# Block 1's attention scores: queries stacked as high over low part, keys in both halves of the rows, two products a score for three

## The chip, the core and the metric

The kernel runs on one core of a Trainium2 chip. The core has five engines with a queue of instructions each: TensorE (PE, matrix products, with its weight loads shown apart as PEld), VectorE (DVE), ScalarE (ACT), GpSimd (POOL) and SyncE (SP, which here only issues transfers, DMAs). Engines wait for each other by semaphores. The metric is the device time of one execution in microseconds (us), lower is better.

## What is computed

A transformer block (block 1) and then two layers of a second kind (block 2), on 512 positions of width 1024, all in fp32. The change lies in block 1's attention. Cut to what matters:

```python
z = rms_norm(x, norm_mix) @ w_in
q_a, k_a, v_a, q_b, k_b, v_b, g_a, g_b = split(z)
# A: 8 heads of 64 over 2 key heads, 512 positions, window of 128 to either side
sc = einsum('bqkgd,bskd->bkgqs', qi, ki) * scale - slopes * dist   # masked, with a sink
y_a = softmax(sc) @ vi
# B: 8 heads of 64 with 8 key heads, each position sees 16 columns of every row of an 8 x 64 grid
sc = einsum('bchd,brckhd->bhcrk', qr, kn) * scale + bias
y_b = softmax(sc) @ vn
x = x + (sigmoid(g_a + b) * (y_a @ w_proj_a) + sigmoid(g_b + b) * (y_b @ w_proj_b)) @ w_out
```

## The kernel before, in words

**Precision.** Every fp32 operand of a product is kept as two fp32r numbers, a high part (an ACT copy, rounded) and a low part (DVE: value less high part). A product of two such operands is three matmuls, high x high, high x low and low x high (`PASSES`), added up in PSUM.

**Stages of block 1.** First the projections of x (0 to 109 us in the trace): weight slabs of 256 columns go into two raw buffers (`K.raw`, slab j into buffer j % 2), are split by ACT (L915) and DVE (L1217) into two weight buffers `K.w`, and PE multiplies them (`fm`, L1741). `IN_TILES` lists 18 tiles: four of A's queries (qa), A's values and keys (va, ka), four of B's queries (qb), B's values (vb) and keys (kb). DVE scales each tile into `K.t` (L1256), ACT writes its high part (`in_hi`, L959) and DVE its low part (`in_lo`, L1230), all 128 rows at once. A tile of queries holds two heads: head 2t in rows 0 to 63, head 2t+1 in rows 64 to 127. `K.ka` holds the two key heads of A in the same way, `K.kb` tile t B's key heads 2t and 2t+1.

Then attention (109 to about 210 us), with A's eight heads before B's eight, each in four tiles of 128 queries, 64 tiles in all, numbered n. A tile of A has 256 keys (first and last of a head) or 384, one of B 256. Tile n goes through all engines: PE scores S (`scores(n)`, L1723) into one of two banks; DVE adds the bias and takes the maximum (L1355); ACT exponentiates (L977); DVE takes the reciprocal of the sum (L1361); POOL multiplies by it (L728); PE transposes (L1826); ACT copies the high part (L1015) and DVE makes the low part (L1381); PE multiplies two tiles at once with the values (`values`, L1853, nine matmuls). After a head, ACT (L986) and DVE (L1373) write its output over the queries' tile.

**The order** is written out by hand and fixed on every engine. PE runs scores(n+3), transposes(n), and for odd n the values of tiles n-3 and n-2. DVE runs scores(n+3), for n = 4h+6 the output of head h, the reciprocal of n+2, the low part of n. ACT runs that same output first, then the exponential of n+2, then the high part of n. POOL runs probabilities(n) and, in B's second to seventh head, after each of the first three tiles an addition of B's bias and mask for the next head (L777, `masked`). Scores 0, 1, 2 and 3 are issued around and inside the last projection tile.

The scores multiply with 64 active rows, `r = slice(e * HD, (e + 1) * HD)` with e the parity of the head.

**SP's queue**, in order: slabs 6 to 8, slab 9 (columns GA0), slab 10 (GB0), which waits until slab 8 is split and so raw buffer 0 is free; eight transfers of A's bias (`biasa`, L646), from the third on each waiting for the scores of the head two before; six of B's bias (`rawb`, L632), each waiting for the masks two heads before; then, after all values, the merge's slabs. Slab 10 is split by ACT and DVE in the merge, after attention.

Of the kernel before, what the change touches and what calls it, by code (L numbers as in the profile page):

```python
# [19 lines left out]
P = 128  # L20
# [146 lines left out]
def allocate(nc, ctx, K):  # L167
# [3 lines left out]
    def semaphore(name):  # L171
        return ctx.enter_context(nc.semaphore(name))
# [51 lines left out]
    def at(name, kb, shape, dt, start=None):  # L224
        off = (a0 if start is None else start) + kb * 1024
        return nc.alloc_sbuf_tensor_at(name, shape, dt, offset=int(off))
# [9 lines left out]
    K.rt = at("rt", 6, [P, 2, 2 * P], F32, p0)  # L236

    K.qa = at("qa", 0, [P, 2, HALF, SEQ], F32R)
    K.ka = at("ka", 16, [P, 2, SEQ], F32R)
    K.va = at("va", 20, [P, 2, TT, P], F32R)  # L240
    K.qb = at("qb", 24, [P, 2, HALF, SEQ], F32R)
    K.kvb = at("kvb", 40, [P, 2 * 2 * HALF * SEQ], F32R)
    n = 2 * HALF * SEQ
    K.kb = K.kvb[:, 0:n].rearrange("p (h t s) -> p h t s", h=2, t=HALF)
    K.vb = K.kvb[:, n:2 * n].rearrange("p (h t s) -> p h t s", h=2, t=TT)
# [48 lines left out]
    K.group_lo = semaphore("group_lo")  # L294
    K.fold_ok = semaphore("fold_ok")
    K.va_full = semaphore("va_full")
    K.pt_zero = semaphore("pt_zero")
    K.tile_full = semaphore("tile_full")
    K.tile_out = semaphore("tile_out")
# [89 lines left out]
def in_dest(K, to, part):  # L389

    name, t = to
    if name == "qa":
        return K.qa[:, part, t, :]
    if name == "qb":
        return blocks(K.qb[:, part, t, :])[:, ::-1, :, ::-1]
    if name == "kb":
        return K.kb[:, part, t, :]
    if name == "ka":
        return K.ka[:, part, :]
    if name == "va":  # L400
        return K.va[:, part, :, :]
    return K.vb[:, part, :, t * P:(t + 1) * P]


def in_shape(to, ap):
# [6 lines left out]
def blocks(ap):  # L412


    return ap.rearrange("p (b r c) -> p r b c", r=KH, c=BLOCK)
# [113 lines left out]
def program_sync(nc, sp, K):  # L529
    a = K.a  # L530

    def slab(j, pieces, pairs=None):


        sp.wait_ge(K.w_lo, (j - 1 + QA_MORE if (j - 3).k >= 0 else Num(HALF)).value())
        if pairs is not None:
            sp.wait_ge(K.pv_done, pairs.value())
        inc = 64 // len(pieces(K.raw[:, j % 2, :]))
        for dst, src, *n in pieces(K.raw[:, j % 2, :]):
            sp.dma_start(dst, src).then_inc(K.w_in_sem[j % 2], n[0] if n else inc)  # L540
# [86 lines left out]
    def bias_rows(h):  # L627


        per = (2 * KH - 1) * WINDOW  # L630
        src = bass.AP(K.rows.tensor, h * per, [[WINDOW, KH], [HEADS * per, BLOCK], [1, KH * WINDOW]])
        sp.dma_start(K.rawb[h % 2][:, :, :], src).then_inc(K.biasb_in[h % 2], 16)  # L632
# [4 lines left out]
    for j in range(6, 9):  # L637
        in_slab(j)
    slab(Num(J_MERGE), columns(a["w_in"][0], GA0))
    slab(Num(J_MERGE + 1), columns(a["w_in"][0], GB0))  # L640

    for h in range(HEADS):
        if h >= 2:
            sp.wait_ge(K.s_taken, S_A + TT * (h - 1))
        head = (h % 2) * HALF + h // 2
        sp.dma_start(K.biasa[:, h % 2, :], a["alibi"][head]).then_inc(K.biasa_in[h % 2], 16)  # L646
    for h in range(2, HEADS):
        sp.wait_ge(K.biasb_ok, 3 * (h - 1))
        bias_rows(h)
    sp.wait_ge(K.pv_done, HEADS * TT)  # L650

    for i in range(4):
# [251 lines left out]
def program_act(nc, act, K):  # L904
# [153 lines left out]
    square_of(KT - 1)  # L1058
    def in_hi(k):
        _, _, form, to = IN_TILES[k]  # L1060
        if form == "turn":
            act.wait_ge(K.va_full, turns(k) + 1)
            hi(in_dest(K, to, 0), in_shape(to, K.T[turns(k) % 2][:, :]))
        else:
            act.wait_ge(K.tile_out, Num(G_IN + k + 1).value())
            hi(in_dest(K, to, 0), in_shape(to, in_src(K, k)))
# [145 lines left out]
def program_vector(nc, dve, K):  # L1212
# [230 lines left out]
    def in_lo(k):  # L1443
        _, _, form, to = IN_TILES[k]
        src = K.T[turns(k) % 2][:, :] if form == "turn" else in_src(K, k)
        lo(in_dest(K, to, 1), in_shape(to, src), in_dest(K, to, 0), Num(H_IN + k))

    def in_normed(k):
# [270 lines left out]
def program_pe(nc, pe, K):  # L1719
# [72 lines left out]
    def attention(A, meanwhile=None):  # L1792
# [3 lines left out]
        def scores(n):  # L1796
            t, e, i, b0, b1 = A.where(n)
            h, kind = n // TT % HEADS, A.at(n)
            r = slice(e * HD, (e + 1) * HD)
            w = (b1 - b0) * P  # L1800
            qs = slice(i * P, (i + 1) * P)
            pe.wait_ge(K.s_taken, (S + n - 1).value())
            if kind == "B" and A.at(n - 1) == "A":
                pe.wait_ge(K.split_lo, H_MERGE)
            if kind == "A":
                pairs = [(K.qa[r, p, t, qs], K.ka[r, q, b0 * P:b1 * P]) for p, q in PASSES]
            elif kind == "B":
                keys = [blocks_of(K.kb[r, q, t, :])[:, B_KEYS[i]] for q in range(2)]
                pairs = [(K.qb[r, p, t, qs], keys[q]) for p, q in PASSES]
            else:  # L1810
                if i == 0:
                    pe.wait_ge(K.tile_out, (A.g_qk(h) + 2).value())
                pairs = [(K.qkh[0:QK, h % 2, 0, p, qs], K.qkh[0:QK, h % 2, 1, q, :]) for p, q in PASSES]
            dst = K.S[(S + n) % 2][:, 0:w]
            if kind == "B":
                dst = dst.rearrange("p (o r c) -> p o r c", r=KH, c=BLOCK)
            product(dst, pairs, K.s_full)
# [323 lines left out]
```

## Time and profile before

| | us |
|---|---|
| median of 3 runs | 1511.17 (1510.67 to 1511.65) |
| profiled execution, its own time | 1508.71 |
| its span, first to last instruction | 1506.7 |
| PE busy | 1482.9 (98%) |
| DVE / ACT / POOL busy | 807.1 / 617.9 / 359.5 |
| PE, share of the chain that ended last | 90% |

The profile is of one execution. Its rows give for each group of instructions the engine, the line, what is written and read, the count, and times in us from the start of the span. A row of the timeline merges neighbours of one kind: its length reaches from the start of the first to the end of the last, and since matmuls are pipelined, the start of the next row is the better measure of how long a group held PE. The granted clock is the share of TensorE's full 2.4 GHz.

### The profile page before, as it was taken

The numbers are of one execution on the slowest core, as the hardware profiler recorded it, in microseconds if no ns is written. First come the engines' busy times: TensorE is split into PE (matmuls) and PEld (weight loads), VectorE is DVE, ScalarE is ACT, GpSimd is POOL, SyncE is SP. The second block draws the span as 40 slices with busy tenths as digits, with TensorE's granted clock in tenths as the row PEclk, the third lists the DMA queues.
The fourth block names the chain that finished last, engine by engine and source line by source line (L and its number), as shares of the span: only waits on it lengthen the run. The fifth ranks groups of instructions, "written<-read, shape, count | busy, mean of one in ns | idle before, by whom it ended". The sixth has DMA issues, their size and how long they took to land.

```text
span 1506.7 us, 18810 instructions
## 1 busy us (share of the span) xinstructions
PE 1482.9 (98%) x7141; PEld 1226.0 (81%) x7141; DVE 807.1 (54%) x1318; ACT 617.9 (41%) x947; POOL 359.5 (24%) x362
## 2 busy tenths in 40 slices
PE   9999999999999999999999999999999999999998
PEld 7887788888888888888888777888888878888886
DVE  6447754344443434344578685544446879644344
ACT  5326752233422323234434675332333458533232
POOL 2104540002100000001308495210120747320012
PEclk9999999999999999999999999999999999999999
DMA  6531022323232232323232002323224200232321
GB/s 199 108 95 33 16 63 86 110 85 122 84 112 84 87 108 84 111 84 112 63 112 84 1 1 85 112 84 109 87 73 129 73 13 1 85 112 84 112 84 57
DMA packets 136478, 125.96 MB, mean 84 GB/s; under 512 B 20807, under 2 KB 132687, under 8 KB 136399
## 3 DMA queue, kind: packets, MB, share of 16 engines
q1 hardware_dynamic: 136239, 124.83, 26.6%
q8 instruction: 51, 0.84, 0.2%
q14 instruction: 28, 0.23, 0.0%
q10 hardware_dynamic: 160, 0.07, 0.0%
HBM read 122.75 MB, written 2.39 MB: 83 GB/s over the span
## 4 chain that ended last, share of the span: by engine, by line
PE 90%; DVE 4%; POOL 4%; ACT 1%; issue 1%; DMA 0%; DVEq 0%; ACTq 0%; SPq 0%; POOLq 0%
PE G L1741 73%; PE G L1723 5%; PE S L1723 4%; PE T L1826 2%; PE G L1853 2%; POOL t L728 2%; PE G L1913 1%; DVE sq L1355 1%; PE G L1846 1%; DVE ab L1234 1%; POOL w L838 1%; DVE pt_l L1381 0%; DMA raw<-in_w_in 0%; DVE z L1369 0%; POOL qk L826 0%
## 5 line engine op out<-in xcount | busy, mean ns | idle before, releaser
L1741 PE MATMUL G<-gx,w 128*128 128x512 f32 x3024 | 694.2, 390 | 0.2 <-DVE w L1217 0.2
L1741 PEld LDWEIGHTS G<-gx,w 128*128 128x128 f32 x3024 | 566.6, 188 | 119.9 <-issue 1.9
L1217 DVE TENSOR_TENSOR w<-raw,w 128x2048 fp32r<-128x2048 f32 (+1 forms) x110 | 252.9, 2299 | 224.1 <-ACT w L915 224.1
L915 ACT ACTIVATE w<-raw 128x2048 fp32r<-128x2048 f32 x112 | 211.6, 1889 | 135.4 <-PE G L1741 109.4
L1741 PE MATMUL G<-kvb,w 128*128 128x512 f32 x960 | 218.4, 389 | 0.0
L1741 PEld LDWEIGHTS G<-kvb,w 128*128 128x128 f32 x960 | 180.2, 188 | 37.4
L728 POOL TENSOR_TENSOR t<-t,rden 128x512 f32<-128x512 f32 (+2 forms) x128 | 108.8, 853 | 142.9 <-DVE rden L1361 142.3
L785 POOL TENSOR_TENSOR t<-sig 128x512 f32<-128x512 f32 x24 | 35.3, 1473 | 356.7 <-DVE sig L1429 356.7
L1486 DVE TENSOR_TENSOR x<-G,x 128x512 f32<-128x512 f32 x56 | 38.6, 689 | 115.3 <-PE G L1741 115.3
L977 ACT ACTIVATE t<-sq,nm 128x512 f32<-128x512 f32 (+3 forms) x128 | 80.2, 627 | 23.2 <-DVE nm L1355 22.6
L866 POOL TENSOR_TENSOR sumsq_f<-sumsq_f,sq_f 128x512 f32<-128x512 f32 x7 | 9.1, 1299 | 333.4 <-ACT sq_f L945 333.4
L1741 PE MATMUL G<-m,w 128*128 128x512 f32 x384 | 87.4, 389 | 0.0
L1741 PEld LDWEIGHTS G<-m,w 128*128 128x128 f32 x384 | 72.1, 188 | 15.0
L1256 DVE SCALAR_TENSOR_TENSOR sig<-G,rstd 128x512 f32<-128x512 f32 x48 | 33.0, 687 | 94.5 <-PE G L1741 94.5
L1826 PE MATMUL T<-ident,t 128*128 128x128 f32 x400 | 69.5, 285 | 11.3 <-POOL t L728 11.3
L1826 PEld LDWEIGHTS T<-ident,t 128*128 128x128 f32 x400 | 44.0, 140 | 37.2 <-POOL t L728 23.3
L1022 ACT ACTIVATE sig<-sig,lp 128x512 f32<-128x512 f32 x32 | 23.2, 724 | 107.6 <-DVE sig L1256 107.6
L719 POOL TENSOR_TENSOR sumsq<-sumsq,sq 128x512 f32<-128x512 f32 x28 | 37.7, 1346 | 119.7 <-ACT sq L933 104.2
L1099 ACT ACTIVATE sq<-t 128x512 f32<-128x512 f32 x32 | 20.2, 632 | 110.8 <-DVE t L1509 110.8
L1723 PE MATMUL S<-ab 96*128 96x512 f32 x192 | 57.7, 410 | 0.7 <-DVE nm L1355 0.7
L1381 DVE TENSOR_TENSOR pt<-T,pt 128x256 fp32r<-128x256 f32 (+2 forms) x96 | 50.6, 527 | 8.0 <-ACT pt L1015 5.1
L1429 DVE TENSOR_TENSOR sig<-G,sig 128x512 f32<-128x512 f32 x48 | 32.0, 686 | 40.9 <-PE G L1741 40.9
(228 smaller groups left out, 1761.2 us busy)
## 6 DMA issues: line engine op xcount, KB each, us to landing
raw<-in_w_in SPq DMA_DIRECT2D x98, 512.0 KB, 7.5
raw<-in_w_up SPq DMA_DIRECT2D x32, 512.0 KB
raw<-in_w_down SPq DMA_DIRECT2D x32, 512.0 KB
raw<-in_w_out SPq DMA_DIRECT2D x24, 512.0 KB
raw<-in_w_attn_proj SPq DMA_DIRECT2D x8, 512.0 KB
raw<-in_w_fourier_proj SPq DMA_DIRECT2D x8, 512.0 KB
xin<-in_x SPq DMA_DIRECT2D x4, 512.0 KB, 6.9
raw<-in_w_proj_a SPq DMA_DIRECT2D x8, 256.0 KB
```

Source lines behind the costliest of these rows:

```text
L719: nc.gpsimd.tensor_tensor(K.sumsq[:, :], K.sumsq[:, :], K.sq[:, k % 2, :], ALU.add).then_inc(K.sum_ok, 1)
L728: nc.gpsimd.tensor_tensor(p, p, K.rden[:, n % 4:n % 4 + 1].broadcast_to([P, (hi - lo) * P]), ALU.mult).then_inc(K.probs_ok, 1)
L785: nc.gpsimd.tensor_tensor(K.t[:, m, :], sig[:, m, :], sig[:, 2 + m, :], ALU.add).then_inc(K.mix_ok, 1)
L915: nc.scalar.activation(K.w[:, j % 2, 0, 0:n], K.raw[:, j % 2, 0:n], ACT.Copy).then_inc(K.w_hi, 1)
L977: nc.scalar.activation(K.t[:, n % 3, 0:width], K.sq[:, n % 2, 0:width], ACT.Exp, bias=K.nm[:, n % 4:n % 4 + 1], scale=-1.0, accum_out=K.de ...
L1217: nc.vector.tensor_tensor(K.w[:, s, 1, 0:n], K.raw[:, s, 0:n], K.w[:, s, 0, 0:n].bitcast(F32), ALU.subtract).then_inc(K.w_lo, 1)
L1256: part = nc.vector.scalar_tensor_tensor(out=dst, in0=src, scalar=scale, in1=rstd, op0=ALU.mult, op1=ALU.mult)
L1381: nc.vector.tensor_tensor(K.pt[A.at(n)][m % 2][:, 1, b0:b1, e, :], K.T[(U + n) % 2][:, 0:(b1 - b0) * P].rearrange("p (k c) -> p k c", c=P) ...
L1486: nc.vector.tensor_tensor(K.x[:, k, :], psum(g)[:, :], K.x[:, k, :], ALU.add).then_inc(K.tile_out, 1)
L1723: mm = nc.tensor.matmul(bank, lhs, rhs, start=(i == 0), stop=(i == len(pairs) - 1))
L1741: mm = nc.tensor.matmul(b[:, :], w(p, k), x(q, k), start=(k == i == 0), stop=(k == kts - 1 and i == len(PASSES) - 1))
L1826: mm = nc.tensor.transpose(K.T[(U + n) % 2][:, k * P:(k + 1) * P], K.t[:, n % 3, c:c + P], K.ident[:, :])
```

## The change

Queries are stored in another way: for head 2t+e, `qsa[:, e, t, :]` (and `qsb`) holds its 64 high-part rows in its own half of the 128 rows and its 64 low-part rows in the other half. ACT and DVE write them with two instructions of 64 rows each for one of 128. The keys of each head are copied by transfers inside SBUF so that both halves of the rows hold the same 64: even heads in `ka1` and `kb1`, odd heads in `ka` and `kb`. A score is then two matmuls with 128 active rows, stacked queries x high keys and stacked queries x low keys; this adds the product low x low, which the kernel before leaves out.

`ka1` takes part of raw buffer 0 and `kb1` weight buffer 0. So slab 10 moves in SP's queue to after the scores of A (and after two of B's biases). The copies of ka go where it was (two of 256 KB, then a third after them), once slab 8 is split. The copies of kb are in four pieces t, two transfers of 256 KB and a third after them, between the A biases. PE waits for `ka1` before score 0, for `ka` before score 4 and for all of `kb` before B's first score. The outputs still go to `K.qa` and `K.qb`, which lie at the same place.

```diff
@@ -236,10 +236,14 @@
     K.rt = at("rt", 6, [P, 2, 2 * P], F32, p0)
 
     K.qa = at("qa", 0, [P, 2, HALF, SEQ], F32R)
+    K.qsa = at("qsa", 0, [P, 2, HALF, SEQ], F32R)
     K.ka = at("ka", 16, [P, 2, SEQ], F32R)
+    K.ka1 = at("ka1", 0, [P, 2, SEQ], F32R, raw0)
     K.va = at("va", 20, [P, 2, TT, P], F32R)
     K.qb = at("qb", 24, [P, 2, HALF, SEQ], F32R)
+    K.qsb = at("qsb", 24, [P, 2, HALF, SEQ], F32R)
     K.kvb = at("kvb", 40, [P, 2 * 2 * HALF * SEQ], F32R)
+    K.kb1 = K.w[:, 0, :, :].rearrange("p h (t s) -> p h t s", t=HALF)
     n = 2 * HALF * SEQ
     K.kb = K.kvb[:, 0:n].rearrange("p (h t s) -> p h t s", h=2, t=HALF)
     K.vb = K.kvb[:, n:2 * n].rearrange("p (h t s) -> p h t s", h=2, t=TT)
...
@@ -400,6 +404,21 @@
     if name == "va":
         return K.va[:, part, :, :]
     return K.vb[:, part, :, t * P:(t + 1) * P]
+def in_halves(K, to, src):
+    name, t = to
+    q = {"qa": K.qsa, "qb": K.qsb}[name]
+    for e in range(2):
+        r, other = slice(e * HD, (e + 1) * HD), slice((1 - e) * HD, (2 - e) * HD)
+        hi, lo = q[r, e, t, :], q[other, e, t, :]
+        if name == "qb":
+            hi, lo = blocks(hi)[:, ::-1, :, ::-1], blocks(lo)[:, ::-1, :, ::-1]
+        yield hi, lo, in_shape(to, src[r, :])
 def in_shape(to, ap):
...
@@ -637,16 +656,54 @@
     for j in range(6, 9):
         in_slab(j)
     slab(Num(J_MERGE), columns(a["w_in"][0], GA0))
-    slab(Num(J_MERGE + 1), columns(a["w_in"][0], GB0))
-
-    for h in range(HEADS):
+    def doubled(keys, keys1, keys_in, keys1_in):
+        for r in range(2):
+            sp.dma_start(keys1[r * HD:(r + 1) * HD].bitcast(F32), keys[0:HD].bitcast(F32)).then_inc(keys1_in, 16)
+        sp.wait_ge(keys1_in, 32)
+        sp.dma_start(keys[0:HD].bitcast(F32), keys[HD:P].bitcast(F32)).then_inc(keys_in, 16)
+    def kb_doubled(t):
+        if t:
+            sp.wait_ge(K.kb1_in, 32 * t)
+            sp.dma_start(K.kb[0:HD, :, t - 1, :].bitcast(F32), K.kb[HD:P, :, t - 1, :].bitcast(F32)).then_inc(K.kb_in, 16)
+        if t < HALF:
+            for r in range(2):
+                sp.dma_start(K.kb1[r * HD:(r + 1) * HD, :, t, :].bitcast(F32),
+                             K.kb[0:HD, :, t, :].bitcast(F32)).then_inc(K.kb1_in, 16)
+    def bias_a(h):
         if h >= 2:
             sp.wait_ge(K.s_taken, S_A + TT * (h - 1))
         head = (h % 2) * HALF + h // 2
         sp.dma_start(K.biasa[:, h % 2, :], a["alibi"][head]).then_inc(K.biasa_in[h % 2], 16)
-    for h in range(2, HEADS):
+    def bias_b(h):
         sp.wait_ge(K.biasb_ok, 3 * (h - 1))
         bias_rows(h)
+    for h in range(2):
+        bias_a(h)
+    sp.wait_ge(K.split_lo, H_IN + 1 + [t[3][0] for t in IN_TILES].index("ka"))
+    sp.wait_ge(K.w_lo, J_MERGE + QA_MORE)
+    doubled(K.ka, K.ka1, K.ka_in, K.ka1_in)
+    for h in range(2, HEADS):
+        bias_a(h)
+        if h == 2:
+            sp.wait_ge(K.split_lo, H_MERGE)
+        if h - 2 <= HALF:
+            kb_doubled(h - 2)
+    for h in range(2, 4):
+        bias_b(h)
+    sp.wait_ge(K.s_taken, S_B)
+    slab(Num(J_MERGE + 1), columns(a["w_in"][0], GB0))
+    for h in range(4, HEADS):
+        bias_b(h)
     sp.wait_ge(K.pv_done, HEADS * TT)
     for i in range(4):
...
@@ -1058,7 +1115,12 @@
     square_of(KT - 1)
     def in_hi(k):
         _, _, form, to = IN_TILES[k]
-        if form == "turn":
+        if form == "q":
+            act.wait_ge(K.tile_out, Num(G_IN + k + 1).value())
+            for high, _, src in in_halves(K, to, in_src(K, k)):
+                part = nc.scalar.activation(high, src, ACT.Copy)
+            part.then_inc(K.split_hi, 1)
+        elif form == "turn":
             act.wait_ge(K.va_full, turns(k) + 1)
             hi(in_dest(K, to, 0), in_shape(to, K.T[turns(k) % 2][:, :]))
         else:
...
@@ -1443,6 +1505,12 @@
     def in_lo(k):
         _, _, form, to = IN_TILES[k]
         src = K.T[turns(k) % 2][:, :] if form == "turn" else in_src(K, k)
+        if form == "q":
+            dve.wait_ge(K.split_hi, H_IN + k + 1)
+            for high, low, of in in_halves(K, to, src):
+                part = nc.vector.tensor_tensor(low, of, high.bitcast(F32), ALU.subtract)
+            part.then_inc(K.split_lo, 1)
+            return
         lo(in_dest(K, to, 1), in_shape(to, src), in_dest(K, to, 0), Num(H_IN + k))
     def in_normed(k):
...
@@ -1800,13 +1868,19 @@
             w = (b1 - b0) * P
             qs = slice(i * P, (i + 1) * P)
             pe.wait_ge(K.s_taken, (S + n - 1).value())
+            if kind == "A" and n == 0:
+                pe.wait_ge(K.ka1_in, 32)
+            if kind == "A" and n == TT:
+                pe.wait_ge(K.ka_in, 16)
             if kind == "B" and A.at(n - 1) == "A":
                 pe.wait_ge(K.split_lo, H_MERGE)
+                pe.wait_ge(K.kb_in, 16 * HALF)
             if kind == "A":
-                pairs = [(K.qa[r, p, t, qs], K.ka[r, q, b0 * P:b1 * P]) for p, q in PASSES]
+                keys = K.ka if e else K.ka1
+                pairs = [(K.qsa[:, e, t, qs], keys[:, q, b0 * P:b1 * P]) for q in range(2)]
             elif kind == "B":
-                keys = [blocks_of(K.kb[r, q, t, :])[:, B_KEYS[i]] for q in range(2)]
-                pairs = [(K.qb[r, p, t, qs], keys[q]) for p, q in PASSES]
+                keys = K.kb if e else K.kb1
+                pairs = [(K.qsb[:, e, t, qs], blocks_of(keys[:, q, t, :])[:, B_KEYS[i]]) for q in range(2)]
             else:
                 if i == 0:
                     pe.wait_ge(K.tile_out, (A.g_qk(h) + 2).value())
```

The rest of the diff makes four semaphores (ka1_in, ka_in, kb1_in, kb_in) and drops the two query cases of `in_dest`.

## Rows read from the trace of the kernel before

**Rows 1.** The page's busy times: us, share of the span, instructions
```profile
PE 1482.9 (98%) x7141; PEld 1226.0 (81%) x7141; DVE 807.1 (54%) x1318; ACT 617.9 (41%) x947; POOL 359.5 (24%) x362
```

**Rows 2.** Busy time by stretch: four heads of A, six heads of B
```profile
128.26:153.72 25.46, 25.46 (x161) 19.98 (x160) 19.87 (x77) 18.75 (x53) 11.48 (x17) 1.00 0.15 43
...
166.14:201.06 34.92, 34.92 (x230) 27.96 (x229) 24.46 (x103) 24.89 (x79) 25.21 (x42) 1.00 0.06 16
```

**Rows 3.** Timeline, PE, block 2: scores of 96 rows; 384 columns at full height
```profile
902.70 0.86 PE L1723 MATMUL S<-ab 96*128 96x512 f32 x3
...
903.40 0.60 PE L1826 MATMUL T<-ident,t 128*128 128x128 f32 x4
...
903.84 1.04 PE L1789 MATMUL G<-ident,qk 128*96 128x128 f32 x8
...
905.41 0.60 PE L1826 MATMUL T<-ident,t 128*128 128x128 f32 x4
...
906.80 0.40 PE L1723 MATMUL S<-ab 96*128 96x512 f32 x1
...
770.82 3.46 PE L1723 MATMUL G<-w,u 128*128 128x384 f32 x19
```

**Rows 4.** Groups that use tile S, B's scores: ns minimum/median/maximum
```profile
L1723 PE MATMUL S<-kvb,qb x96: 273/282/386, 161.0 to 207.2; 64*128 64x256 f32 x96
```

**Rows 5.** Timeline, PE, in a head of A, stretch 132.4 to 139 us
```profile
133.19 0.44 PE L1826 MATMUL T<-ident,t 128*128 128x128 f32 x2
...
134.63 0.62 PE L1723 MATMUL S<-ka,qa 64*128 64x256 f32 x3
...
135.18 0.44 PE L1826 MATMUL T<-ident,t 128*128 128x128 f32 x2
...
136.10 0.55 PE L1826 MATMUL T<-ident,t 128*128 128x128 f32 x3
...
137.64 0.79 PE L1723 MATMUL S<-ka,qa 64*128 64x384 f32 x3
```

**Rows 6.** Timeline, one loop in a head of B with masks
```profile
174.85 0.63 PE L1723 MATMUL S<-kvb,qb 64*128 64x256 f32 x3
...
175.66 0.42 DVE L1355 CUSTOM_DVE_ANT_0 sq<-S,biasb 128x256 f32<-128x256 f32 x1 [0.92 <-PE S L1723]
...
176.83 0.61 POOL L728 TENSOR_TENSOR t<-t,rden 128x256 f32<-128x256 f32 x1 [1.14 <-DVE rden L1361]
...
178.11 0.61 POOL L728 TENSOR_TENSOR t<-t,rden 128x256 f32<-128x256 f32 x1
```

**Rows 7.** Timeline, the same loop in a head of A, from DVE on
```profile
151.20 0.62 DVE L1355 CUSTOM_DVE_ANT_0 sq<-S,biasa,sink 128x384 f32<-128x384 f32 x1 [0.64 <-PE S L1723]
...
152.88 0.60 DVE L1355 CUSTOM_DVE_ANT_0 sq<-S,biasa,sink 128x384 f32<-128x384 f32 x1
...
153.64 0.82 POOL L728 TENSOR_TENSOR t<-t,rden 128x384 f32<-128x384 f32 x1 [0.45 <-DVE rden L1361]
```

**Rows 8.** Timeline, projections: queries' high part, slab 3's split, its first product
```profile
36.34 0.64 ACT L959 ACTIVATE qa<-t 128x512 fp32r<-128x512 f32 x1 [0.77 <-DVE t L1256]
...
40.00 2.29 DVE L1217 TENSOR_TENSOR w<-raw,w 128x2048 fp32r<-128x2048 f32 x1 [1.90 <-ACT w L915]
...
46.70 15.48 PE L1741 MATMUL G<-gx,w 128*128 128x512 f32 x67
```

**Rows 9.** Transfers: slab 10's issue, first scores, a busy stretch, landings by kind
```profile
102.84 0.94 SPq L540 DMA_DIRECT2D raw<-in_w_in  x2
...
108.91 1.14 PE L1723 MATMUL S<-ka,qa 64*128 64x256 f32 x6
...
105.00:107.00 2.00, 2.00 (x10) 1.66 (x9) 0.34 (x1) 2.00 (x2) 0.00 (x0) 1.00 1.04 369
...
raw<-in_w_in SPq DMA_DIRECT2D x98, 512.0 KB, 7.5
...
out<-xout SPq DMA_DIRECT2D x4, 512.0 KB, 2.7
```

More of the change, by code:

```diff
@@ L296, in allocate @@
     K.va_full = semaphore("va_full")
+    K.ka1_in = semaphore("ka1_in")
+    K.ka_in = semaphore("ka_in")
+    K.kb1_in = semaphore("kb1_in")
+    K.kb_in = semaphore("kb_in")
     K.pt_zero = semaphore("pt_zero")
@@ L391, in in_dest @@
     name, t = to
[L392 to L395, printed above, removed]
     if name == "kb":
```

## The prediction

> **What bounds the kernel now.** I read the page's busy table first: TensorE (PE) is busy for 98% of the span, every other engine 54% or less [rows 1]. So only what shortens PE's own queue, or makes PE wait, can move the end. The change touches block 1's attention; the busy table by stretches shows it. Over four A heads (25.46 us, 6.365 us a head) and over six B heads (34.92 us, 5.82 us a head) PE is busy all the time at a granted clock of 1.00, while DVE needs 4.97 and 4.08 us a head, ACT 4.69 and 4.15, POOL 2.87 and 4.20 (each row's busy time over 4 or 6) [rows 2]. PE is the limit there, but with only 1.4 to 1.6 us a head in hand before another engine is. The whole stage runs from about 109 to 210 us.
>
> **Inside a head** a tile is scores (S), then transposes of older probabilities (T), and after every second tile the products with the values (V). I take the pitch of full-height products from stretches where PE never stalls: four transposes last 0.44 us (0.109 each) [rows 3], four transposes and eight 256-column products 1.39 us, so 0.119 for one of 256; nineteen of 384 columns span 3.46 us, or 0.177 each with the last one's tail of 0.28 [rows 4] off; three score products with 96 rows and 512 columns take 0.70 us from their start to the next transposes, which is their bare length (0.23 each) [rows 3]. In the changed stage the distances are longer than such pitches. From T x2 plus V x9 to the next score: 1.44 us, where 2 x 0.109 + 9 x 0.119 = 1.29. From a score of three 256-column products to the transposes: 0.55, where 3 x 0.119 = 0.36 [rows 5]. So each score with 64 active rows costs 0.15 + 0.19 = 0.34 us beyond its columns: PE stalls going into and out of the 64-row products. Scores of 96 rows do not show it [rows 3]. Inside the group one product spans 0.62 in all and lasts 0.28 alone [rows 4, 5], so the starts lie 0.34 apart where 2 x 0.119 = 0.24 was due: 0.10 of the stall is between the first two products.
>
> That this goes with the change is a conclusion, since no row shows 128-row scores here; the nearest rows are the 96-row ones, and they stall by nothing [rows 3]. The Trainium skill (TensorEngine Tiling (Array Packing), Tiling Modes, Key Properties) says that changing the tiling mode, such as between 64-row and full-height tiles, drains TensorE. By that rule the stall goes wholly with the change, as I assume from the rows; the trace agrees by its 0.34 us at 64 rows and none at 96.
>
> **Part by part.**
> 1. One product fewer in each of 64 scores. 48 have 256 columns, 16 have 384: 48 x 0.119 + 16 x 0.177 = 8.5 us of PE time.
> 2. The stall: 64 x 0.34 = 21.8 us of PE time; bounds 0 (it belongs to something else) and 21.8. I take all of it, by the 96-row rows.
> PE alone would then need 4 T-groups (10 x 0.109), 18 x 0.119, and 4 x 0.119 + 4 x 0.177 in an A head = 4.41 us, and 8 x 0.109 + 18 x 0.119 + 8 x 0.119 = 3.97 in a B head. It can't have that; what comes late next is a loop through other engines.
> 3. The next limit in **A**. Once a head, DVE's queue holds: scores of tile n+3, the output of the head before (L1373), the reciprocal (L1361) of n+2, the low part of n, scores n+4, reciprocal of n+3. POOL waits for that reciprocal, PE's T(n+3) for POOL, the next head's V for T, and V stands before the score that DVE waits for. Its length: T x3 to the next score 1.54 us now [rows 5], 3 x 0.109 + 9 x 0.119 + 0.05 = 1.45 after; score to DVE 0.81 [rows 6], less the third product and the 0.10 = 0.53; DVE's two scores 1.68 apart, then 0.76 to POOL [rows 7]; POOL 0.82, and 0.05 to PE. Sum 5.29 us against 6.365: 1.07 a head.
> 4. In **B** the masks go between the probabilities on POOL (L777): T to score 1.44 now [rows 5], 1.34 after; score to DVE 0.81, less 0.22 = 0.59; DVE to POOL 1.17; the two probabilities with a mask between them 1.28; POOL 0.61 and 0.05 to PE [rows 6]. Sum 5.04 against 5.82: 0.78 a head. B's first and last head have no masks; there I take 1.4 and 1.0.
> 5. Start of the stage: scores 0 to 3 stand between projection products on PE, in its queue alone. Scores 0 and 1 follow each other, so it is three stalls and four products, 3 x 0.34 + 2 x 0.119 + 2 x 0.177 = 1.6; the head after only fills the pipeline, and I take 1.0 there.
> The sum: 1.6 + 1.0 + 6 x 1.07 + 1.4 + 6 x 0.78 + 1.0 = **16.1 us**.
> 6. Query tiles in two halves: ACT and DVE each run two instructions of 64 rows for one of 128. Rows don't shorten an instruction, so eight tiles cost each engine about 0.6 us more (0.63 on ACT) [rows 8], 4.8 us in all. PE's projection products cover it. The tightest place is the four qa tiles: ACT's and DVE's four halves go ahead of the split of slab 3, which DVE ends at 42.29 and PE needs at 46.70 [rows 8]; 4 x 0.6 = 2.4 leaves 2.0. Cost 0; with the cover gone it would be at most 0.4 (2.4 on each of ACT and DVE, less 4.4).
> 7. SP's queue: the GB0 slab goes behind the A scores; its split in the merge comes some 50 us after its new issue. Cost 0. The first two biases go earlier. Each copy of keys is an issue on SP of some 0.5 us, in a queue that otherwise waits.
> 8. The key copies. ka's first two (256 KB each, 64 rows) can start when slab 8 is split: SP issues the GB0 slab at 102.84 now [rows 9], and the copies take its place. They are due at 108.91, when scores 0 start [rows 9]: 6 us. No row copies SBUF to SBUF; a transfer of 512 KB out of SBUF lands after 2.7 us, slab transfers after 7.5 [rows 9]. Between 2.7 and 7.5 the cost is 0 to 1.5 us, and for the third copy, due about 7 us later, 0 to 3. I take 0, by the row whose source is SBUF. PE's new waits stand at the head of its queue, so a late copy would hold all of it, and with it DVE and ACT. The B keys (four pieces of 768 KB) have from about 121 us to the end of A, over 30 us.
> So 1508.71 - 16.1 = 1492.6 for the profiled execution; that one lies 2.46 below the median of the runs, 1511.17, and so the time is **1495.1**.
>
> **The rivals.**
> A. The stall stays: it belongs to the wait in front of the scores or to switching operands, not to 64 rows. For it: PE does wait on a semaphore there. Against: the 96-row scores have the same wait and no stall [rows 3]. PE then needs 6.365 - 0.59 in A and 5.82 - 0.48 in B, above the loops: 8.5 us saved, 1502.7. Chance 0.12.
> B. The loops do not bind, engines' sums do: 4.97 (DVE) in A, 4.20 (POOL) in B [rows 2]. Then 1.6 + 1.0 + 6 x 1.39 + 1.5 + 6 x 1.62 + 1.0 = 23.2 us, 1488.0. For it: the buffers are three tiles deep. Against: the order on each engine is fixed and DVE's output instruction stands ahead of the reciprocal. Chance 0.15.
> C. Slower than before: the copies inside SBUF are slow, and B's scores wait for them. After the last query tile is split SP has 3.1 MB of B keys and 1.0 MB of A biases to move in about 32 us, so it costs nothing above 128 GB/s; to eat the 16 us it must be below 4.1 MB / 48 us = 85 GB/s. At the rate of the slab transfers, 512 KB in 7.5 us or 70 GB/s [rows 9], it takes 59 us: 27 us of waiting, 11 us slower, 1522. For it: 64 partitions only, and biases queue behind keys. Against: the queue moved 369 GB/s from 105 to 107 us, and the 7.5 is mostly measured with many transfers in flight [rows 9]. Chance 0.06.
> D. Full-height weight loads are exposed, and not the 64-row ones. A load takes at least 0.125 us (PEld 19.98 us busy for 160 loads [rows 2]). Outside each of the new products it would bring PE to 4.41 + 8 x 0.125 = 5.41 and 3.97 + 1.00 = 4.97 us a head, beside loops of about the same length: 15 us saved, 1496, hardly another result. At twice that, 6.4 and 5.97, nothing would be left but the start: 1510. Against: the nine products of V have 128 rows, and their loads are hidden (0.119 apart [rows 3]). Chance 0.03, at 1510. The Trainium skill (TensorE: Matmul & The Clock Gate, Part 3, The mechanism) says that weight loads overlap running products only where their row groups differ, which speaks for D; the trace contradicts it here with that 0.119.
>
> **How the numbers follow.** The forecast (13 to 19 us saved, 1492 to 1498) has 0.64, A 0.12, B 0.15, C 0.06, D 0.03. The range leaves out C and D and the far end of both sides: from B with a little more, 1487, to A with late first copies (+1.5), 1504. A measurement of this kernel tells about 0.2%, 3 us, from no change. Faster by over 0.2%: forecast, A and B, 0.91. Within 0.2%: 0.03 (D, or C just at its turning point). Slower: 0.06.
>
> **What would show it.** Right: scores of two products with 128 active rows, 0.24 or 0.35 us long up to the transposes and no stall on either side; heads of about 5.3 and 5.0 us; PE idle about 0.9 us a head, ended by POOL's L728; the stage about 16 us shorter and the rest as before. A would show as distances of 0.15 and 0.19 above the pitches with PE still busy all the time. B as heads below 5. C as PE idle before the first score, the fifth or the first B score, ended by a DMA. Wrong would be the prediction, too, if the projection stage (34 to 109 us) grew: then point 6 failed.

## The result

Over four runs of each kernel on one chip, the changed kernel took 1499.59 us (1498.41 to 1501.03) and the kernel before 1510.92 us (1509.06 to 1511.65). The ratio is 0.9928, with a 95% interval of 0.9914 to 0.9942: faster by 11.3 us, or 0.7%. The forecast was 1495.1 us, with a range of 1487 to 1504. The execution profiled after took 1498.41 us and has a span of 1496.6 us (before: 1508.71 and 1506.7).

### The profile page after: what moved, and what is told of

The parts are those of the page before. It is cut to its first block, busy times and chain, and to the rows that moved or that the text cites. A ratio compares the mean times of both kernels' runs of the same rounds, so it can differ in the third digit from the quotient of the medians.

```text
span 1496.6 us, 18716 instructions
## 1 busy us (share of the span) xinstructions
PE 1460.6 (98%) x7077; PEld 1216.7 (81%) x7077; DVE 812.8 (54%) x1326; ACT 620.9 (41%) x955; POOL 359.4 (24%) x362
## 4 chain that ended last, share of the span: by engine, by line
PE 86%; POOL 5%; DVE 5%; issue 2%; ACT 1%; DVEq 0%; ACTq 0%; POOLq 0%
PE G L1809 75%; PE G L1791 5%; POOL t L785 3%; PE S L1791 2%; DVE sq L1417 1%; PE G L1987 1%; PE T L1900 1%; PE G L1920 1%; DVE ab L1296 1%; PE G L1927 1%; POOL w L895 1%; POOL biasb L834 1%; DVE pt_l L1443 0%; DVE z L1431 0%; DVE pt L1443 0%
```

## The profile after

The page's busy times after the change (us, share of the span, instructions), to be read beside [rows 1]:

```profile
PE 1460.6 (98%) x7077; PEld 1216.7 (81%) x7077; DVE 812.8 (54%) x1326; ACT 620.9 (41%) x955; POOL 359.4 (24%) x362
```

PE has 64 products fewer and is busy for 22.3 us less. The span is 10.1 us shorter. So about half of the busy time that PE lost came back as waiting.

Busy time by stretch, over four A heads and then six B heads (us of the stretch; busy of PE, PEld, DVE, ACT, POOL; granted clock; DMA share; GB/s):

```profile
131.12:153.18 22.06, 19.92 (x146) 17.64 (x145) 19.77 (x77) 17.61 (x53) 11.49 (x17) 1.00 0.48 119
159.22:190.29 31.07, 26.58 (x207) 24.07 (x205) 24.70 (x104) 24.81 (x80) 25.55 (x42) 1.00 0.08 21
```

Beside [rows 2], four A heads fell from 25.46 to 22.06 us and six B heads from 34.92 to 31.07. The other engines run the same instructions as before, give or take one at the edges of a stretch. (ACT's busy time in A reads 17.61 for 53 instructions, where it was 18.75. The lengths of its instructions add up to 21.8 and 22.0; their records overlap more when they follow each other closely.) PE, busy throughout before, now stands still for 2.1 us in the first stretch and 4.5 us in the second.

PE's timeline in the A section (start us, duration us, engine, line, instruction, out<-in, tiling, shape, count, and in brackets the wait):

```profile
125.78 0.40 PE L1791 MATMUL S<-ka,qsa 128*128 128x256 f32 x2
...
126.05 0.44 PE L1900 MATMUL T<-ident,t 128*128 128x128 f32 x2
...
127.33 0.55 PE L1900 MATMUL T<-ident,t 128*128 128x128 f32 x3 [0.48 <-POOL t L785]
...
127.64 1.32 PE L1927 MATMUL G<-pt,va 128*128 128x256 f32 x9
...
128.79 0.52 PE L1791 MATMUL S<-ka,qsa 128*128 128x384 f32 x2
...
129.15 0.49 PE L1900 MATMUL T<-ident,t 128*128 128x128 f32 x3
...
129.82 0.38 PE L1900 MATMUL T<-ident,t 128*128 128x128 f32 x2
...
131.12 0.40 PE L1791 MATMUL S<-ka,qsa 128*128 128x256 f32 x2
```

The stall is gone on both sides. A 256-column score reaches its transposes after 0.27 us (126.05 - 125.78; the two products alone are 0.24), where [rows 5] had 0.55 for three. T x2 and V x9 reach the next score after 1.30 us (131.12 - 129.82), where [rows 5] had 1.44. A 384-column score takes 0.36 (2 x 0.177 = 0.35). PE now waits 0.48 us for POOL's probabilities before T, once a head.

The stage itself, from the start of the first score to the start of the last product with the values (the last accumulation), is the cleanest measure of the change. Around it executions of the same kernel differ: the first score came anywhere from 108.8 to 111.8 us in the traces of this study, and the span went on for between 4.4 and 7.3 us after PE's last product. Before, the stage lasted from 108.91 to 212.47, or 103.55 us unrounded; after, from 109.12 to 200.58, or 91.46. It lost 12.1 us. The span shows only 10.1, mainly because it went on for 5.6 us after DVE's last instruction this time, against 3.2 before. Only the output's transfers are left there.

The distances from one head's fourth score to the next head's tell where the gain lies. Before: 5.30, then six A heads of 6.36 or 6.37. After: 4.62, 5.61, 5.33, 5.71, 5.32, 5.71, 5.32. In the B section I take the distances of the heads' first scores. Before: 6.04, then 5.80 to 5.84. After: 5.08, 5.04, 5.32, 5.05, 5.31, 5.04, 5.31. **Every second head meets the forecast loops (5.29 and 5.04). The ones between are 0.38 and 0.27 us longer**, which the prediction did not have. (The 5.61 is a shift of the score within its first turn: from T to T, 122.00 to 127.33, that turn takes 5.33.)

DVE in such a long head:

```profile
129.35 0.62 DVE L1417 CUSTOM_DVE_ANT_0 sq<-S,biasa,sink 128x384 f32<-128x384 f32 x1 [0.29 <-PE S L1791]
...
129.89 0.08 DVE L1417 DVE_READ_ACCUMULATOR2_ANT nm<- 128x1 f32 x1
...
130.00 0.69 DVE L1435 TENSOR_TENSOR qa<-G,qa 64x512 fp32r<-64x512 f32 x1
...
130.73 0.16 DVE L1423 RECIPROCAL rden<-den 128x1 f32<-128x1 f32 x1
130.93 0.56 DVE L1443 TENSOR_TENSOR pt<-T,pt 128x384 fp32r<-128x384 f32 x1
...
131.40 0.61 DVE L1417 CUSTOM_DVE_ANT_0 sq<-S,biasa,sink 128x384 f32<-128x384 f32 x1
```

DVE's two scores are 2.05 us apart. The forecast had 1.68, from [rows 7]. What differs from head to head between them is the place of the output (L1435). It lies on rows 64 to 127 for odd heads and on rows 0 to 63 for even ones.

## The experiments

Two theories had to be told apart from their rivals: that the gain comes from the height of the products, and that the long heads come from the rows of the output. Two more questions were what limits the stage now, and whether the key copies cost anything. All times of the stage are from the first score to the last accumulation.

**1. Two products of 64 rows.** On the kernel before:

```diff
-                pairs = [(K.qa[r, p, t, qs], K.ka[r, q, b0 * P:b1 * P]) for p, q in PASSES]
+                pairs = [(K.qa[r, p, t, qs], K.ka[r, q, b0 * P:b1 * P]) for p, q in PASSES[:2]]
```

and the same for the B keys.

> The kernel before with two of block 1's three products a score (high with high, query high with key low); the third, query low with key high, is left out, so the scores are coarser. The two products still read 64 rows. Theory (the product read from 64 rows among full-height ones is what costs the stall of about 0.34 us a score): the stalls stay, only 128 streams go; a head of the A section gets about 0.59 us shorter than 6.36 (5.8), one of the B section 0.48 shorter than 5.82 (5.34), and the whole about 8 us shorter than before, 1503. Rival (the saving of the change is that of the third product alone, wherever the operands lie): the heads come down to those of the changed kernel, 5.5 and 5.2 on average, and the whole to 1499.6.

Measured: 1504.37 us, ratio 0.9957 (0.9940 to 0.9974). The stage was 96.57 us. Even A heads took 5.77 and even B heads 5.34 us, as the theory of the stall has them; odd ones took 5.91 and 5.48. PE's rows:

```profile
131.80 0.44 PE L1826 MATMUL T<-ident,t 128*128 128x128 f32 x2
...
133.23 0.50 PE L1723 MATMUL S<-ka,qa 64*128 64x256 f32 x2
133.66 0.44 PE L1826 MATMUL T<-ident,t 128*128 128x128 f32 x2
```

A score of two products reaches T after 0.43 us, not 0.24, and T x2 with V x9 reaches it after 1.43, not 1.29. Both halves of the stall, 0.19 and 0.14, are there with two products as with three.

**2. Three products of 128 rows.** On the kernel before:

```diff
-                pairs = [(K.qa[r, p, t, qs], K.ka[r, q, b0 * P:b1 * P]) for p, q in PASSES]
+                pairs = [(K.qa[:, p, t, qs], K.ka[:, q, b0 * P:b1 * P]) for p, q in PASSES]
```

and the same for the B keys.

> The kernel before with its three products a score, each over all 128 rows (the features of both heads of a pair are summed, so the scores are not those of the reference); no key copies, no two-way query splits. Theory (the rows are what counts): the 0.34 us a score vanish although the number of products is that of before; the loop through the vector and pool engines grows by one product a score, so that heads come to about 5.50 and 5.88 us in the A section and 5.16 and 5.43 in the B section, in turn, and the whole to about 1501.5, 2 us above the changed kernel. Rival (the third product, not the rows, is what was saved): heads of 6.36 and 5.82 as before, 1510.9.

Measured: 1499.06 us, ratio 0.9927 (0.9910 to 0.9943). A heads took 5.49 and 5.90 in turn, and B heads settled at 5.14 to 5.17 and 5.40 to 5.47. The stage was 93.75 us, 2.3 above the changed kernel's. The whole did not show those 2 us; executions differ by as much. PE's rows:

```profile
132.08 0.52 PE L1723 MATMUL S<-ka,qa 128*128 128x256 f32 x3
132.44 0.43 PE L1826 MATMUL T<-ident,t 128*128 128x128 f32 x2
```

Three products reach T after 0.36 us, which is 3 x 0.119 to the hundredth. The two runs settle it. Of the 12.1 us, the height alone gives 9.8 (103.55 - 93.75), and the third product alone gives 7.0 (103.55 - 96.57). Together they would be 16.8, more than the whole. They do not add up, because the loop through DVE and POOL takes over before PE's gain is used up. In experiment 1 the odd heads already lie 0.14 us above the even ones, in experiment 2 PE waits for POOL.

**3. No key copies.** On the changed kernel:

```diff
-    doubled(K.ka, K.ka1, K.ka_in, K.ka1_in)
...
-        if h - 2 <= HALF:
-            kb_doubled(h - 2)
...
-                keys = K.ka if e else K.ka1
+                keys = K.ka
```

with the B keys alike, and without PE's three waits.

> The changed kernel without the key copies between the bias transfers and without the waits on them: the even heads read the undoubled keys in the same tiles, so that half their scores' terms are wrong. Theory (the copies lie beside other work and nothing waits for them): 1499.6 within 1 us. Rival (copies delay the bias transfers or the first heads): 2 us or more faster than the changed kernel, with the B section's first heads closer together.

Measured: 1498.62 us, ratio 0.9921 (0.9904 to 0.9937). The stage was 91.45 us, where the changed kernel has 91.46, with the same heads to 0.03 us. The copies cost nothing.

**4. The kernel before with late outputs.** This moves one call in each of two queues; DVE's is shown, and ACT's (`out_hi`) goes behind its `pt_hi` in the same way:

```diff
-            if A.last_of(n) is not None:
+            if A.last_of(n) is not None and A.kind == "L":
                 ...
+            if A.last_of(n - 1) is not None and A.kind != "L":
+                out(A.last_of(n - 1))
```

> The kernel before with one thing moved: a head's division and high part (vector engine's output, scalar engine's high part) at the end of the next step, after that step's low part, in block 1; the numbers are the same. Theory (before, the heads go at the tensor engine's pace, so the loop through the vector engine is no limit): the time of before, 1510.9 within 1 us. Rival (the loop already limited before, and the stalls of 0.34 us are only where the slack shows): 3 us or more faster.

Measured: 1509.26 us, ratio 0.9994 (0.9984 to 1.0003), over ten runs. The stage was 103.56 us, with every head as before. Before the change PE set the pace, and the loop did not.

**5. The changed kernel with late outputs.** The same edit.

> The changed kernel with a head's division and high part moved, in block 1, from between a step's scores and its low part to the end of the next step; the numbers are the same. Theory (after the change, block 1's heads go by the loop of scores, mask, exponential, low part and accumulation, and the output instructions lie in it once a head): the A section's heads come down to about 4.75 to 4.9 us, the B section's to 4.5 to 5.0 where the vector engine is busy nearly throughout, and the whole to about 1491 to 1494. Rival (an engine's sum is already the limit): less than 2 us.

Measured: 1491.19 us, ratio 0.9869 (0.9852 to 0.9885). A heads took 4.99 us each after the first two; B heads 4.49 and 4.77 in turn. The stage was 84.19 us, 7.3 below the changed kernel. So the loop with the output in it was what the stage waited for. The A heads stay a little above the 4.75 to 4.9 that I expected. Busy times over four A heads, and then over nearly five B heads:

```profile
128.03:148.00 19.97, 18.59 (x147) 17.53 (x146) 19.14 (x76) 17.55 (x54) 11.47 (x16) 1.00 0.58 148
161.50:184.00 22.50, 20.29 (x167) 19.26 (x166) 19.72 (x83) 20.30 (x65) 21.80 (x35) 1.00 0.10 24
```

In A, DVE is busy for 19.14 of 19.97 us. In B, POOL is, for 21.80 of 22.50. Its four probabilities of 0.61 and three masks of 0.74 make 4.66 us a head, a little too much because their records overlap, and the heads take 4.63 on average. Engines' sums, the limit of rival B, decide only now.

**6. Masks later.** On the changed kernel, in POOL's queue:

```diff
-                if b // TT + 1 >= 2 and b // TT + 1 < HEADS and b % TT < 3:
-                    masked(b // TT + 1, b % TT)
+                if b // TT + 2 < HEADS and b % TT:
+                    masked(b // TT + 2, b % TT - 1)
```

> The changed kernel with the pool engine's masks of the B section issued one probability tile later, two heads ahead, so that none lies between the probabilities of the steps that the loop runs through; the numbers are the same. Theory (in the B section the vector engine's square waits for the mask, 4.7 us in all): the B heads lose part of that, 4.5 to 4.9 us instead of 5.04, 1 to 3 us in all, 1497 to 1498.6. Rival (pool is the pace of the B section with its 25.3 of 30.8 us): no change.

Measured: 1495.55 us, ratio 0.9903 (0.9886 to 0.9919). The whole looks 4 us better, but the stage was 90.89 us, only 0.6 less. The six full B heads took 31.00 us against 31.07: 5.29 and then 5.14 or 5.15 each, not 4.5 to 4.9. In its trace the span ends 3.2 us after DVE's last instruction, as in the kernel before, and not 5.6.

My mechanism for a real gain failed, and it rested on a wait that I had misread. In the changed kernel's B section the profile puts DVE's wait before a head's second score down to POOL's third mask:

```profile
176.84 0.74 POOL L834 TENSOR_TENSOR biasb<-rawb,mask 128x256 f32<-128x256 f32 x1
...
177.03 0.40 PE L1791 MATMUL S<-w,qsb 128*128 128x256 f32 x2
...
177.60 0.42 DVE L1417 CUSTOM_DVE_ANT_0 sq<-S,biasb 128x256 f32<-128x256 f32 x1 [0.61 <-POOL biasb L834]
```

The mask ended at 177.58, just before. But by the program (`B_BIAS`) a head's second score needs only its second mask, which had ended at 176.31. The score waited for PE: it starts 0.58 us after PE's in each of the B heads, and experiment 8 has the same 0.58 with the last mask over a microsecond away.

**7. Both moves.**

> The changed kernel with both moves: outputs late, masks off the loop; the numbers are the same. If both terms stand and no engine's sum stops them: A heads 4.75 to 4.9 us, B heads 4.45 to 4.7, in all about 1489 to 1492. If the vector engine's sum stops the B section: as with the outputs late alone.

Measured: 1495.61 us, ratio 0.9895 (0.9879 to 0.9912). The stage was 88.31 us, 4.1 longer than with the outputs alone. The A heads kept their 4.99; the B heads rose to 5.17 and 5.45. Waits in the B section of this run (engine, line, what it waited for: us in total, times, longest):

```profile
PEld T L1904 <- POOL t L785: 7.8, 12, 0.8
...
POOL biasb L834 <- DVE nm L1419: 4.8, 6, 1.0
```

The second row has no like in the changed kernel's B section. Two heads ahead, a mask writes the bias buffer that the current head's scores still read. So POOL stands still up to 1.0 us for DVE, and the probabilities queue behind it. The trace of experiment 6 has the same wait, 3.3 us in five. I had taken the mask out of one loop and put it into another. It remained to show that the mask in its old place costs anything.

**8. Short masks.** On the changed kernel, the masks of heads 2 to 7 in their old places, cut to a few columns each:

```diff
-        nc.gpsimd.tensor_tensor(K.biasb[:, h % 2, v, :].rearrange("p (o r c) -> p o r c", r=KH, c=BLOCK), raw, near,
+        bias = K.biasb[:, h % 2, v, :].rearrange("p (o r c) -> p o r c", r=KH, c=BLOCK)
+        c = slice(0, 1 if h >= 2 else BLOCK)
+        nc.gpsimd.tensor_tensor(bias[:, :, :, c], raw[:, :, :, c], near[:, :, :, c],
                                 ALU.add).then_inc(K.biasb_ok, 1)
```

> The changed kernel with the pool engine's mask instructions of the B section in their places but cut to two columns of 256 (heads 2 to 7 keep old biases elsewhere, so their outputs are wrong). Theory (a mask of 0.74 us stands in the loop of a B head, which is why moving it into the path of another wait won nothing): B heads fall from 5.04 and 5.31 by most of 0.74 us, to 4.4 to 4.7, and the stage from 91.46 by 3 to 4.5 us. Rival (the pool engine's masks lie beside the loop, and the moved masks cost nothing either way): B heads of 5.04 and 5.31 as in the changed kernel.

The profile calls the short form 128x16; the cut left 16 columns of 256, not 2. It lasts 0.228 us against 0.737, half a microsecond less. Measured, in one run of 1496.74 us: a stage of 88.66 us, 2.8 below, and B heads of 4.64 where the changed kernel has 5.31 or 5.32, and 4.77 or 4.78 where it has 5.04 or 5.05, once the short masks begin: over these five heads 0.51 less on average. That is one mask's difference a head, though three masks a head were shortened. It fits the prediction's point 4, in whose loop one mask lies and the other two do not. DVE's score still starts 0.58 us after PE's:

```profile
177.58 0.24 POOL L836 TENSOR_TENSOR biasb<-rawb,mask 128x16 f32<-128x16 f32 x1
...
178.27 0.40 PE L1793 MATMUL S<-w,qsb 128*128 128x256 f32 x2
...
178.85 0.42 DVE L1419 CUSTOM_DVE_ANT_0 sq<-S,biasb 128x256 f32<-128x256 f32 x1 [0.60 <-PE S L1793]
```

One mask shortened by itself was not tried. With the masks short the heads still alternate, and why the long ones gain 0.67 us and the short ones 0.27 is open. The stage fell a little less than the 3 to 4.5 us I expected, since I had counted on 0.74 a head, not 0.51.

**9. All outputs on rows 0 to 63.** On the changed kernel, in ACT's `out_hi` and DVE's `out`:

```diff
-            r = slice(e * HD, (e + 1) * HD)
-            q = K.qa if A.at(h * TT) == "A" else K.qb
+            r = slice(0, HD)
+            q = K.qsa if A.at(h * TT) == "A" else K.qsb
```

> The changed kernel with the odd heads' outputs divided, split and stored in rows 0 to 63 like the even heads' (in other tiles; the output of block 1 is then wrong for the odd heads). Theory (the long heads, 5.71 against 5.33 us in the A section and 5.31 against 5.04 in the B section, are long because two instructions of each on rows 64 to 127 add about 0.12 us of idle time before and after themselves): the odd heads come down to 5.33 and 5.04, 7 x 0.38 + 6 x 0.27 = about 4 us at the most off the stage, 1495.5 to 1497. Rival (the alternation comes from the head's number, its bias buffers or its keys' copies): no change, 1499.6, and the alternation stays.

Measured: 1497.12 us, ratio 0.9906 (0.9890 to 0.9923). The stage was 89.15 us, 2.3 below the changed kernel. The A heads took 5.32 each after the first two, and the last four full B heads 5.04 to 5.07. The same instructions as in the long head above:

```profile
131.30 0.62 DVE L1417 CUSTOM_DVE_ANT_0 sq<-S,biasa,sink 128x384 f32<-128x384 f32 x1 [0.28 <-PE S L1791]
131.84 0.08 DVE L1417 DVE_READ_ACCUMULATOR2_ANT nm<- 128x1 f32 x1
131.84 0.68 DVE L1435 TENSOR_TENSOR qsa<-G,qsa 64x512 fp32r<-64x512 f32 x1
132.44 0.14 DVE L1423 RECIPROCAL rden<-den 128x1 f32<-128x1 f32 x1
132.51 0.53 DVE L1443 TENSOR_TENSOR pt<-T,pt 128x384 fp32r<-128x384 f32 x1
132.97 0.60 DVE L1417 CUSTOM_DVE_ANT_0 sq<-S,biasa,sink 128x384 f32<-128x384 f32 x1
```

The output lasts the same, 0.68 against 0.69. But it starts with its predecessor's last record, not 0.11 us after it; the reciprocal follows its start by 0.60, not 0.73, and the low part follows the reciprocal by 0.07, not 0.20. 0.11 + 0.13 + 0.13 = 0.37 us, and a long A head has 0.38 over a short one. In a B head only the first two lie on the way from DVE's score to POOL: 1.43 us in a long head, 1.18 in a short one, and the heads differ by 0.27.

The edit moves ACT's half of the output too, and ACT's rows show such gaps as well. In the long head of the changed kernel:

```profile
128.99 0.59 ACT L1043 ACTIVATE qa<-G 64x512 fp32r<-64x512 f32 x1 [0.58 <-PE G L1927]
129.61 0.51 ACT L1034 ACTIVATE t<-sq,nm 128x257 f32<-128x257 f32 x1
130.03 0.19 ACT L1034 ACTIVATION_READ_ACCUMULATOR t<-sq,nm 128x1 f32 x1
130.24 0.49 ACT L1072 ACTIVATE pt<-T 128x384 fp32r<-128x384 f32 x1
```

From the output to the next start it is 0.62 us, and from the accumulator to the high part 0.21; with the output on rows 0 to 63 it is 0.50 and 0.09. DVE's low part waits for that high part. In the changed kernel it does not wait long: the high part ends at 130.73 and the low part starts at 130.93. But without DVE's own gaps the low part could have started at 130.56 (129.89 + 0.60 + 0.07), and ACT would have held it until 130.73. So DVE's gaps set the 0.37, and by this estimate ACT's alone would still cost 0.17 of it. No run moves one without the other.

**10. All outputs on rows 64 to 127.** The same edit with `r = slice(HD, P)`.

> The changed kernel with the output instructions of all heads of block 1 on rows 64 to 127 (the counterpart of the run with all of them on rows 0 to 63; the outputs are wrong). Theory (rows 64 to 127 cost the extra time, whichever head it is): every head takes the long time, 5.71 us in the A section and about 5.3 in the B section, the stage from the first score to the last accumulation is 91.46 + 3 x 0.38 + 3 x 0.27 = 93.4 us. Rival (it is the alternation itself, a change of rows from one head to the next): every head takes the short time, 5.32 and 5.04, as with all on rows 0 to 63, 89.15 us.

Measured, in one run of 1502.33 us: a stage of 93.78 us (expected 93.4), and A heads of 5.71 or 5.72 after the first two. B heads after the first two took 5.33, 5.27, 5.32, 5.28 and 5.30. Each head is long. The rows themselves cost the time, and not the change from one half to the other.

## Why the prediction was right, and where it was off

The direction and the mechanism held, and 1499.59 lies in the range of 1487 to 1504. But the saving in the stage was 12.1 us where the sum said 16.1, below the 13 to 19 to which the prediction gave 0.64. It fell between that and rival A. By its own steps:

- **Points 1 and 2 (the product and the stall)** held. Score to transposes is 0.27 and 0.36 us; T x2 with V x9 to the next score is 1.30. Experiments 1 and 2 tie the stall to the 64 rows. Both agree with the rule of the Trainium skill that the prediction named (TensorEngine Tiling (Array Packing), Tiling Modes, Key Properties), that a change of tiling mode drains TensorE.
- **Point 3 (the loop in A)** held for even heads: 5.32 to 5.33 against 5.29. By its terms, in the short head after the long one: T x3 to score 1.45 (forecast 1.45), score to DVE 0.56 (0.53), DVE's scores 1.66 apart (1.68), then 0.77 to POOL (0.76), POOL to T 0.88 (0.87). The term that failed is the third, for odd heads: 2.05 us. I had read it from one head in [rows 7], and that was one with its output on rows 0 to 63. The delays were in the kernel before too, where PE's queue covered them. The six heads saved 5.2 us, not 6.4.
- **Point 4 (the loop in B)** failed in the same place, its term from DVE to POOL: 1.18 us in even heads (forecast 1.17) and 1.43 in odd ones. The heads are 5.04 or 5.05, as forecast, and 5.31 or 5.32. The six gave 3.9 us, not 4.7.
- **Point 5 (start)**: from score 0 to score 3 the time fell from 7.68 to 6.43, 1.25 against 1.6. That sum counted the last score's product, and its stall in full, which fall into the next head. The head after that gave 0.68 (forecast 1.0), the first B head 0.96 (1.4), and the last heads, with the step from A to B, 0.2 in place of 1.0. The last 1.0 was a guess without a row, and the trace shows why it was too high: after the last score a chain of single steps runs to the last accumulation. It takes 5.60 us before and 5.64 after, so it gained nothing from the change.
- **Point 6 (queries in halves)** held. Slab 3's split ends at 45.77 on DVE, and PE starts on it at 47.00:

```profile
43.48 2.29 DVE L1279 TENSOR_TENSOR w<-raw,w 128x2048 fp32r<-128x2048 f32 x1 [1.86 <-ACT w L972]
...
46.41 1.39 DVE L1511 TENSOR_TENSOR qsa<-t,qsa 64x512 fp32r<-64x512 f32 x2
...
47.00 3.24 PE L1809 MATMUL G<-gx,w 128*128 128x512 f32 x13
```

  The cover that was 4.4 us [rows 8] is 1.2 now, where the prediction had left 2.0. It still cost nothing: PE is busy throughout from 34 to 109 us, and the first score comes 0.2 us later than before, no more than slab 3's first product already did (0.3).
- **Points 7 and 8 (SP's queue, the copies)** held, shown by experiment 3. The copies' rows in the list of transfers issued from 100 to 125 us (KB each, median us to landing):

```profile
ka<-ka SPq DMA_DIRECT2D x3, 256.0 KB, 3.0
w<-kvb SPq DMA_DIRECT2D x3, 256.0 KB, 3.7
```

  3.0 us lies near the 2.7 taken, and far from 7.5. Later copies of kb took up to 4.9.

The sign "PE idle about 0.9 us a head" came out at 0.5 in A and 0.75 in B, ended by POOL's probabilities as said. The record of a group counts the tail of its last product as busy (the score of 0.24 us at 126.35 stands there as 0.50), so a part of the standing still does not show.

By term, the measured saving is 1.25 + 0.68 + 5.2 + 0.96 + 3.9 + 0.2 = 12.2, against 12.1 seen directly. Of the 4 us that were missing, 2.0 are in the twelve full heads and 1.9 in the start, the first heads and the end. The 2.0 are the odd heads' outputs (2 x 0.38 + 3 x 0.27 = 1.6), the shift of the first turn (0.3) and small differences in the loops' other terms.

The rivals: A (the stall stays) fell in experiment 2 and in the changed kernel itself. B (only engines' sums bind) fell in the changed kernel's heads, and its numbers came near once experiment 5 opened the loop: 4.99 and 4.63 us a head against its 4.97 and 4.20. C fell in experiment 3. D fell by PE's distances of 0.27 and 0.36 us from score to transposes.

The kernel of experiment 5 beats both: 1491.19 us, 0.9869 of the kernel before. What stays open is why A's heads don't alternate in experiment 5 while B's do.

## What to carry to other kernels

Sum each engine's work, and then follow the loop that a tile makes through all engines. Once the busiest engine was relieved here, only 12 of its 22 us came out, and the next step was to move two instructions out of that loop, not to make any of them shorter. Read a loop term from two neighbouring periods, not from one. Where an engine waits for several semaphores, the one that the profile names only came last: look up in the program which one was needed. And before moving an instruction out of one queue's critical place, look up who still reads the buffer that it writes.

## What the hardware showed that was not expected

- The outputs, instructions of 64 rows on ACT and DVE, last the same on rows 64 to 127 as on rows 0 to 63 (0.59 us on ACT, 0.68 to 0.69 on DVE). On DVE, though, an output on the upper rows adds 0.11 us before it, 0.13 after it, and 0.13 more one instruction later: 0.37 us in all, while the instructions around it are the same. Experiments 9 and 10 show it on all heads at once, in both directions. In the long head each of the three starts 0.03 to 0.04 us after the recorded end of its predecessor (130.00 after 129.97, 130.73 after 130.69, 130.93 after 130.89); in the short head each starts before that end. The Trainium skill has a model that fits (VectorE: DVE Perf Modes, Two Vector instructions with no wait between them): an instruction starts only after all earlier ones have finished when one of its inputs or its output begins in another group of 32 partitions than the last one in the same memory. By it three instructions are held here: the output (its operands begin at row 64), the reciprocal behind it (back to row 0 in SBUF), and the low part (back to row 0 in PSUM, which the reciprocal didn't read). The trace has just three delays, at these three places. That it is this mechanism was not tried by itself. ACT shows two gaps of 0.12 us around its output on the upper rows, and what causes those stays open.
- A score of 64 rows among full-height products costs PE 0.14 us on entering and 0.19 on leaving, for two products as for three. With 128 rows both are within 0.03 of zero (experiment 2 and the changed kernel).
- Where an edit had no effect on it, the stage's length came out the same to 0.01 us (103.55 and, in experiment 4, 103.56; 91.46 and, in experiment 3, 91.45), while whole times of one kernel differ by 2 to 3 us. For edits of a microsecond the stage in the trace is the better ruler.
